# Turnings of block one moved inside its products, the final norm folded into the next projection, and the third and fourth mixed groups turned half a step later

## What is computed

```python
def first_block(x, ...):
    for l in range(DEPTH):                       # DEPTH = 2
        h = rms_norm(x, norm_mix[l])
        proj = h @ w_in[l]                       # q, k, v of two attentions, and the gates
        ...
        y_a = dilated_attention(dq, dk, dv) @ w_proj_a[l]
        y_b = stick_breaking_attention(sq, sk, sv) @ w_proj_b[l]
        gates = jax.nn.sigmoid(gate_logits + b_gate[l])
        mixed = gates[..., :D_MODEL] * y_a + gates[..., D_MODEL:] * y_b
        x = x + mixed @ w_out[l]
        h = rms_norm(x, norm_ffn[l])
        x = x + conv_ffn(h, w_up[l], conv_w[l], conv_b[l], w_down[l])
    return rms_norm(x, norm_final)

def second_block(x, mem, ...):
    for l in range(DEPTH):
        h = rms_norm_2(x, g[0])
        y = even_mixer(h, ...) if l % 2 == 0 else odd_mixer(h, ...)    # both start with h @ w_in
        x = x + rms_norm_2(y, g[1])
        ...                                      # memory attention, then the MLP, each with its norms
```

## Time and profile before

| what | us |
|---|---|
| median of 3 timed runs | 1427.8 |
| lowest, highest | 1427.16, 1429.24 |
| the profiled execution, its own time | 1425.17 |
| its span in the trace | 1423.4 |
| PE busy | 1391.6 (98% of the span) |
| DVE busy | 1014.5 (71%) |
| ACT busy | 739.5 (52%) |
| POOL busy | 85.8 (6%) |

### The profile page before, as it was taken

The page is one execution under the profiler, slowest core; times in us unless marked ns, Lnnn a source line. Parts: engine busy times, 40 slices in busy tenths (PEclk is TensorE's granted clock), DMA queues, the critical chain, the costliest instruction groups (busy, mean ns, idle before and its releaser), DMA issues.

```text
span 1423.4 us, 20307 instructions
## 1 busy us (share of the span) xinstructions
PE 1391.6 (98%) x7929; PEld 1188.1 (83%) x7929; DVE 1014.5 (71%) x1523; ACT 739.5 (52%) x1130; POOL 85.8 (6%) x94
## 2 busy tenths in 40 slices
PE   8999999999999999999999999999999999999997
PEld 6899888888788987888888777888888878888886
DVE  5566678777665657977787667787667866886665
ACT  4563455555445554555455555554444664654443
POOL 0000001000000000211111003000000000000000
PEclk9999999999999999999999999999999999999999
DMA  8844355555465334666656323448875423365652
GB/s 298 249 129 149 119 177 195 190 178 192 163 208 177 119 119 150 217 191 213 210 190 192 115 79 106 147 164 229 205 217 193 170 97 103 107 206 180 204 191 75
DMA packets 154434, 242.36 MB, mean 170 GB/s; under 512 B 4506, under 2 KB 107050, under 8 KB 154076
## 3 DMA queue, kind: packets, MB, share of 16 engines
q1 hardware_dynamic: 150624, 227.23, 49.1%
q0 software_dynamic: 3712, 13.84, 3.8%
q10 hardware_dynamic: 4, 0.01, 0.0%
HBM read 239.09 MB, written 1.97 MB: 169 GB/s over the span
## 4 chain that ended last, share of the span: by engine, by line
PE 91%; DVE 5%; ACT 2%; POOL 1%; issue 1%; DMA 0%; SPq 0%; DVEq 0%; ACTq 0%; POOLq 0%
PE ps L938 19%; PE ps L904 16%; PE ps L911 16%; PE ps L908 16%; PE ps L941 10%; PE ps L1013 3%; PE ps L1091 2%; PE ps L1067 2%; PE ps L1082 1%; DVE wlo L2067 1%; PE ps L977 1%; PE ps L978 1%; PE ps L979 1%; DVE x L2483 0%; PE ps L1527 0%
## 5 line engine op out<-in xcount | busy, mean ns | idle before, releaser
L2067 DVE TENSOR_TENSOR wlo<-raw,whi 128x1024 fp32r<-128x1024 f32 (+1 forms) x432 | 539.2, 1259 | 205.0 <-ACT whi L1615 204.4
L1615 ACT CAST whi<-raw 128x1024 fp32r<-128x1024 f32 (+1 forms) x432 | 446.4, 1042 | 276.7 <-PE ps L911 173.8
L938 PE MATMUL ps<-act,whi 128*128 128x512 f32 x1184 | 324.9, 395 | 1.2 <-DVE wlo L2067 0.9
L904 PE MATMUL ps<-whi,mhi 128*128 128x512 f32 (+2 forms) x688 | 236.4, 392 | 4.0 <-DVE mlo L2091 2.2
L938 PEld LDWEIGHTS ps<-act,whi 128*128 128x128 f32 x1184 | 204.8, 189 | 31.9 <-DVE wlo L2067 1.6
L911 PE MATMUL ps<-whi,mlo 128*128 128x512 f32 (+2 forms) x688 | 231.4, 385 | 0.0
L908 PE MATMUL ps<-wlo,mhi 128*128 128x512 f32 (+2 forms) x688 | 231.1, 385 | 0.0
L941 PEld LDWEIGHTS ps<-act,wlo 128*128 128x128 f32 x1184 | 182.6, 189 | 25.7
L941 PE MATMUL ps<-act,wlo 128*128 128x256 f32 x1184 | 189.3, 281 | 0.0
L904 PE MATMUL ps<-whi,act 128*128 128x256 f32 (+1 forms) x512 | 169.2, 330 | 1.5 <-DVE act L2094 1.5
L908 PE MATMUL ps<-wlo,act 128*128 128x256 f32 (+1 forms) x512 | 165.5, 323 | 0.0
(11 more groups left out here) (266 smaller groups left out, 1471.1 us busy)
## 6 DMA issues: line engine op xcount, KB each, us to landing
raw<-in_mlp_w SPq DMA_DIRECT2D x64, 1024.0 KB, 5.3
raw<-in_w_up SPq DMA_DIRECT2D x44, 1024.0 KB, 5.2
raw<-in_w_in SPq DMA_DIRECT2D x39, 1024.0 KB, 5.2
raw<-in_w_down SPq DMA_DIRECT2D x22, 1024.0 KB, 4.8
raw<-in_ev_w_in SPq DMA_DIRECT2D x10, 1024.0 KB, 5.1
raw<-in_w_out SPq DMA_DIRECT2D x8, 1024.0 KB, 5.0
raw<-in_xa_wkv SPq DMA_DIRECT2D x4, 1024.0 KB, 5.3
raw<-in_ev_w_out SPq DMA_DIRECT2D x4, 1024.0 KB, 5.0
```

Source lines behind the costliest of these rows:

```text
L904: nc.tensor.matmul(o, hi[:, kx, rows_], wh[:, k, c0:c0 + w], start=first and h == 0 and k == 0 and (tt == 0 or at[1] == 0), stop=False)
L938: nc.tensor.matmul(both, wh[:, k, w], act2[:, kx].rearrange("p i n -> p (i n)"), start=kx == 0, stop=False)
L1615: nc.scalar.copy(whi[:, m % HL, 0:w], raw[:, n % RAW, h * w:h * w + w]).then_inc(hi_done, 1)
L2067: nc.vector.tensor_tensor(wlo[:, m % HL, 0:w], raw[:, n % RAW, h * w:h * w + w], whi[:, m % HL, 0:w].bitcast(F32), ALU.subtract).then_inc( ...
```

## The change

1. **Branch a turned inside `pb`.** `turn_branch("a")` stands after the first row tile of the second half of `pb`. ACT runs both sigmoids first, then a weight half, then takes branch a. DVE takes branch a's low part between its two `gate_b` operations on the first columns, and puts the second column's two `gate_b` operations later, the last of them after the first two mixed groups.
2. **Mixed groups.** The stream `mix` turns one group less ahead: groups 0 and 1 together as before, the third in the middle of the second half of `out1`'s first job, the fourth before its third half. (Before: third after the first half, fourth after the second.)
3. **Next layer's first groups.** Groups 0 and 1 of `x1` of layer 1 are turned inside the last `down` of layer 0, in the middle of its second 512 columns; ACT and DVE take their parts there, DVE each one between the additions to `x`.
4. **Final norm folded.** For layer 0 of block two PE turns the `x` that is not yet normed, between the two halves of the memory projection; the gain row is the product of both gains (`gains_joined`, made once at the start by DVE), and the root is the product of the final norm's root and the root of the normed `x` (`x2 alone`), which POOL multiplies. DVE norms `x` itself later, behind the four groups' low parts, tile by tile with the squares. One more row of gains is loaded and turned at the start (17 rows for 16).

In the tables below, the line numbers of the changed kernel are its own: L1022 turns (L1013 before), L910, L914, L917 are `half_chunk`'s products (L904, L908, L911), L984 to L986 `column_chunk`'s (L977 to L979), L2089 is DVE's pass over a half of the weights (L2067), L2116 the low part of a scaled group (L2094), L2489 the final norm (L2461), L2139 the squares (L2117).

PE at the branch products of block one, before: `whi,mhi`, `wlo,mhi`, `whi,mlo` with x2 are `pb`, `cst,o_nat` is the turning of branch a, L977 the first product of `pa`.

The diff, cut to what the prediction speaks of:

```diff
@@ def build_network
-    GAIN_ROWS = 18
+    GAIN_ROWS = 19
+    FINAL_ROW = GAIN_ROWS - 1
@@ @block.sync
                     sp.dma_start(gain_rows[14:16, :], a["xa_mem_norm_2"]).then_inc(rows_in, 16)
+                    sp.dma_start(gain_rows[16:17, :], a["norm_final"].unsqueeze(0)).then_inc(rows_in, 16)
@@ @block.gpsimd
-            root(("x2", 0), 2)
+            root(("x2 alone", 0), 2)
+            pool.wait_ge(rstd_ready, rs_count["x2 alone", 0])
+            nc.gpsimd.tensor_tensor(rstd[:, NORM["x2", 0], 0:TT], rstd[:, NORM["x2 alone", 0], 0:TT], rstd[:, NORM["final",], 0:TT],
+                                    ALU.mult).then_inc(rstd_ready, 1)
@@ @block.tensor, column_chunk
+                        if inside and c == 1 and h == 0:
+                            inside()
@@ between_heads
-                        half_chunk(plan.jobs["pb", l][0], h, mhi, mlo, 2, [...], True, True)
+                        half_chunk(plan.jobs["pb", l][0], h, mhi, mlo, 2, [...], True, True,
+                                   middle=attended if h else None)
...
-                pe.wait_ge(o_ready, o_counts["dil", l])
-                turn_branch("a")
...
-                sx = stream("mix", l, o_nat, lambda h: pe.wait_ge(mixed, 4 * l + 2 * h + 2))
+                sm = stream("mix", l, o_nat, lambda h: pe.wait_ge(mixed, 4 * l + 2 * h + 2), ahead=1)
+                sm["turn_to"](1)
...
-                wide_job(("out1", l, 0), mhi, mlo, [yb(0, 0), yb(1, 0)], stream=sx)
+                wide_job(("out1", l, 0), mhi, mlo, [yb(0, 0), yb(1, 0)], stream=sm,
+                         middles={1: lambda: sm["turn_to"](2)}, before={2: lambda: sm["turn_to"](3)})
@@ down
-                    tall_job(("down", l, b), mhi, mlo, 2 * (b % 4), lambda tt, c: yb(tt, c), b == 0, b == NFB - 1)
+                    tall_job(("down", l, b), mhi, mlo, 2 * (b % 4), lambda tt, c: yb(tt, c), b == 0, b == NFB - 1,
+                             inside=(lambda: sx["turn_to"](1)) if l + 1 < DEPTH else None)
@@ second block
-                if l:
-                    sx["turn_to"](1)
+                sx["turn_to"](1)
@@ @block.scalar
-                nc.scalar.activation(gates[:, :, D:2 * D], gates[:, :, D:2 * D], ACT.Sigmoid).then_inc(gate_done, 1)
+                for c0 in (D, 0):
+                    nc.scalar.activation(gates[:, :, c0:c0 + D], gates[:, :, c0:c0 + D], ACT.Sigmoid).then_inc(gate_done, 1)
+                split_half(f0 + 2 * NGC + 4)
                 take(("y1", l, "a"), blocks(mhi, 0))
                 split_half(f0 + 2 * NGC + 5)
-                nc.scalar.activation(gates[:, :, 0:D], gates[:, :, 0:D], ACT.Sigmoid).then_inc(gate_done, 1)
...
+                else:
+                    split_half(n0 + 3)
+                    stream_hi("x1", l + 1, ahi, row=gain_row["x1", l + 1], gs=(0, 1))
...
                 if l == 0:
-                    memory_product(l, "v", 6)
+                    act.wait_ge(gains_joined, 1)
                 stream_hi("x2", l, mhi, row=gain_row["x2", l], gs=(0, 1))
-                if l:
-                    memory_product(l, "v", 6)
+                memory_product(l, "v", 6)
...
+                    if s == 4 and l == 0:
+                        split_half(n0 + 7)
@@ @block.vector
-                n = gate_b(0)
+                gate_b(0, 0)
                 lo_of(("y1", l, "a"), mhi, mlo, 0)
-                n1 = gate_b(1)
+                n = gate_b(0, 1)
                 split_half(f0 + 2 * NGC + 4)
+                gate_b(1, 0)
                 dve.wait_ge(gate_done, 2 * l + 2)
                 gate_a(0, n)
                 split_half(f0 + 2 * NGC + 5)
                 stream_lo("mix", l, mhi, mlo, gs=(0, 1))
-                gate_a(1, n1)
+                n = gate_b(1, 1)
+                gate_a(1, n)
                 split_half(f0 + 2 * NGC + 7)
                 stream_lo("mix", l, mhi, mlo, gs=(2, 3))
...
                     ins.then_inc(x_ready, 1)
+                    if l + 1 < DEPTH:
+                        stream_lo("x1", l + 1, ahi, alo, row=gain_row["x1", l + 1], gs=(c,))
...
+                    for tt in range(TT):
+                        finish_first_block((tt,))
+                        dve.wait_ge(x_ready, x_count("final") - 2 * TT + 2 * tt + 2)
+                        squares(("x2 alone", l), lambda tt: x[:, tt, :], D, (tt,))
+                        split_half(nk + 8 + tt)
```

82 lines of the change are left out of this document (48 added, 34 removed).

## The result

The changed kernel took 1419.54 us (median of 4, 1418.97 to 1420.15), against 1427.48 us of four runs of before: ratio 0.9943, 95% interval 0.9926 to 0.996. The same code measured again took 1419.76 us (5 runs) against 1426.8 (27 runs): 0.9951 [0.9937, 0.9964]. So the step is 7.0 to 7.9 us. The forecast had 6.2 us and 1421.6, with a range from 1419.8; the time lies 0.3 under its low end.

What follows compares the result with a forecast made beforehand. PE was taken as the bound, busy 1391.6 us of 1423.4, so only its waits could shrink. 2 x 1.35 + 2 x 0.1 + 1.35 + 1.97 - 0.05 = 6.2 us off 1427.8 gave 1421.6, range 1419.8 to 1424.4.

Steps and rivals of the forecast that it cites:

- last step of the sum: Whole kernel: took the 6.2 us saving from the timed median of before, 1427.8, giving 1421.6.
- reference: Whole kernel before the change: timed median taken as 1427.8 us, 2.6 above the profiled execution.
- half-step: Block one, `out1`, twice: third and fourth mixed groups turned half a chunk later, 0.1 us each, between -0.4 and 0.25.
- Branch a inside `pb`: Block one, ahead of `pa`, twice: turning ahead of the last six `pb` products starts `pa` 1.35 us earlier.
- Entry of layer 1: Layer 1's first groups turned ahead of the last six products of layer 0's `down`: 1.35 us, once.
- Final norm folded: Entry of block two, once: turnings between the memory projection's halves leave no wait before `in2`, 1.97 us, less 0.05.
- Start: Kernel start: the added gain row, its transfer, turning and small DVE operation run beside other work and cost nothing.
- 0.2 us taken for the multiplication: POOL, behind the root for the first `in2` result: multiplying the two roots takes 0.2 us, with 0.7 kept for the range.
- margin of 0.3 at the ninth half: `in2`: the ninth weight half is ready 0.3 us before PE wants it, or stalls 0.2 with a long multiplication.
- Rival one: `in2` root: POOL is held during DVE's work, the ninth half stalls 1.9 us, time 1423.8; chance 0.13.
- Rival two: At each spot DVE or ACT is later than counted, gains halved: saving 3, 1424.8; chance 0.17, 0.09 of it no change.
- Rival three: `in2` weight ring: a chunk lands over 15 us after issue and PE waits, slower, 1431; chance 0.04.

Runs made afterwards that it cites:

- a_rootlate: The changed kernel with two more powers on POOL ahead of the root of the first `in2` norm, making that root 1.44 us later: 1420.84 us (4 runs).

## Why the prediction was right or wrong

The waits came out nearly as forecast; what failed is the last step of the sum, "against it the same step gives 1427.8 - 6.2 = 1421.6". Its reference was 1.1 us too high, and it had no term for falls of the clock. Of the 2.1 us between 1421.6 and the 1419.5 measured, 1.1 lie in the reference, 0.4 in the parts (the half-step above all), and the last 0.6 go with the clock. The reference alone decides it: from 1426.7 the range would have begun at 1418.7.

**The sum of the parts** was nearly right: 6.2 us forecast, 6.57 between landmarks.
- Branch a inside `pb`, 2 x 1.35: at `pa` the gain is there (wait 0.45 in place of 1.65, 1.31 us in each layer). The 1.35 us are also kept to the start of `out1`, as forecast. But the working stopped there; behind it the third group gives 0.5 us of it back, unless that turning is moved too.
- Half-step, 2 x 0.1: mis-sized, 2 x 0.73 in this kernel. The working took the 0.51 us gap of before as the whole prize; with DVE's new order and the earlier `out1` the gap in the old place would be 1.12. I counted DVE's extra operation against the new place of the turning and forgot it against the old one. Together the two terms came to 2 x 1.45, and 2 x 1.57 was measured, so two errors cancelled.
- Entry of layer 1: 1.35 against 1.38. Final norm folded: 1.97 - 0.05 against 2.05. Start: nothing that shows, as said. The 0.2 us taken for the multiplication and the margin of 0.3 at the ninth half were both right.
- The slips in the working are small: 379.34 stands where 379.32 was worked out, and the root comes to 777.36, not 777.45. The low end of the range, 1419.8, is a saving of 8.0; the bounds and the half microsecond named for it come to 7.5 at the most, so it was drawn wider than worked out and still too high.

**The reference** was the largest miss. The 1427.8 rested on the median of three runs; of 101 later ones it is 1426.7. The step had named the 2.6 us between the profiled execution and that median, and gave no reason for them. Part of them is a drop of the clock that comes or not, and the profiled execution had none in its course. The other 1.1 us came with those three runs: all three took 1427.16 or more, as 21 of the 101 later ones did, and the longest, 1429.24, is above all of these. Whether that was chance or something of that occasion is open. With the later median and the parts as measured the sum gives 1426.7 - 6.57 = 1420.1.

**What the forecast had no term for** is that the clock falls less often in the changed kernel (2 of 9 runs at 0.997, against 67 of 101 of before at 0.996 or 0.997). From 1420.1 to the measured 1419.5 and 1419.8 are 0.6 and 0.3 us: that is the term. In two traces the drop follows the gap that the fold closed, and filling that gap alone lowered the median by 0.9 us, with an interval that holds no change; that the closed gap is the cause of the whole term is likely and not shown.

**The rivals.** Rival one (POOL held by DVE, the root late) did not happen. The issues took 0.53 to 0.63 us and the root 0.72 while DVE's row at 770.93 ran beside the issues; the root itself fell into the time of a DVE memset, not of the weight half. Its consequence (a stall at the ninth half) does follow when the root is late, as `a_rootlate` shows. The Trainium skill, page "SBUF — State Buffer", section "SBUF: two separate sides", has the lock that would hold POOL; the rows here show that it did not reach POOL's issues. No run put the root of `x2 alone` beside a two-input operation; the next root, so placed in `a_rootlate`, took 1.63 us, which agrees with the page. Rival two (gaps come back): it happened at one place, the third group, and the half-step had already paid for it. Rival three (a weight chunk lands late): ACT waited 1.9 us for such a transfer near 782 us, and PE has no wait there.

**What would have shown it**: the waits ahead of `pa`, layer 1 and `in2` came out as written, and no new wait of over 1 us stands on PE in block one or in `in2`. PE's idle time fell from 31.8 to 26.5; 26 was said.

## What to carry to other kernels

When a change reorders an engine's queue, work out the next wait for the old place of every later step too, not only for the new one: what a moved step is worth is measured against what the gap would have become. Before setting a small step against a median, ask what the scatter of that median is made of (here the granted clock of each run tells) and from how many runs it comes. A wait of PE of 2 us between small turnings and the next product may cost more than its width, since the clock can fall behind it (1.6 us, in two of nine traces here). Where it can't be closed, products that nobody reads fill it without a cost here; that they gain anything is likely and not shown.
